# A gather ring of four pairs of rows, with the fifth pair's place left to the first query chunk

## The chip, the cores and the metric

The kernel runs on one core of one Trainium2 chip. The metric is the device time of one execution in microseconds (us), lower is better. Beside the plain runs there is one profiled execution, whose trace gives a start and a duration for every instruction.

## What is computed

Two layers of a hybrid encoder on 256 tokens of 1024 features, in float32, and a final RMS norm. Each layer first adds a mixture of differential attention and a two-directional state-space block to x. Then comes the part on which the change bears, a layer of 128 x 128 = 16384 small experts:

```python
def peer_ffn(h, wq, keys, u_tab, v_tab):
    qry = (h @ wq).reshape(b, s, PEER_HEADS, 2, PEER_HALF)
    sc = jnp.einsum('bshcd,hckd->bshck', qry, keys)
    ...                                    # top 16 of each half, top 16 of their 256 sums: idx, gate
    u = jnp.take(u_tab, ix, axis=0)        # per token 8 heads x 16 = 128 rows
    act = jax.nn.gelu(jnp.einsum('btkd,btd->btk', u, hx), approximate=False)
    wgt = act * gx
    return jnp.einsum('btk,btkd->btd', wgt, jnp.take(v_tab, ix, axis=0))
```

So each of the 256 tokens needs 128 rows of u and 128 rows of v of its own, per layer. They can't be shared, and they all come from HBM.

## The kernel before, in words

Tokens lie on the 128 partitions, in two blocks b = 0 and 1. The tables u and v are put side by side in HBM (peer_uv, 2048 floats a row), so one indirect DMA of GpSimd (POOL) fetches for all 128 tokens of a block the 8 KB row of one of their 128 slots: 1 MiB. Two slots make a **pair**; a block has 64 pairs, a layer 128 (LAYER_PAIRS). The fetched rows go into `ring`, which holds RING_PAIRS = 5 pairs; pair m takes the place m % 5.

Each pair goes through a chain of engines, in the order of m on each:

- POOL issues its two gathers (line 1489), after the index list of the heads is there (experts_ready) and after pair m-5 has been used (pair_used).
- VectorE takes the dot product of each row's u half with h2, one instruction a row (`dots`, line 1379), after both gathers have landed (gathered[q]).
- ScalarE (ACT) applies gelu, the gate, and makes a diagonal matrix from the weights (`weigh`, lines 921, 927, 934).
- TensorE (PE) multiplies the diagonals with the v halves, eight matmuls that add into PSUM (line 693), and reports pair_used.

While pairs flow, VectorE chooses the experts of the heads to come (`route`), in steps between the dots. TensorE computes the queries and key scores that it needs: those of block 0 and the first chunk of block 1 before the first pair (`query_tiles`, line 634, and `key_scores`, line 645), the others (LATE) in pieces behind certain pairs. The order on TensorE at the start of this phase is: query_tiles(0, 1), key_scores(0, 1), the copy of x_tok into PSUM (line 684), then the pairs from 0 on.

The query weights are four chunks of 2 MB. Chunks 1 and 2 pass through the ring of weights w_ring. Chunk 0 (wq0) and chunk 3 (wq3) have places of their own in the arena, a stretch of SBUF that the phases use in turn. wq0 lies 8 x 2 x DM x 4 bytes behind the arena's start, so on the fifth pair's place of the gather ring (16 KB of each partition), and out1 on the fourth pair's. That is why POOL waits before pair 3 for the last product with out1 (mix_full) and before pair 4 for the last use of wq0, the fill of query_tiles(0, 1), which PE reports through bank_full. SP loads wq0 behind the last chunks of the state-space block (line 363) and wq3 at the layer's end (line 370).

Of the kernel before, what the change touches and what calls it, by code (L numbers as in the profile page):

```python
# [20 lines left out]
DEPTH, SEQ, DM = 2, 256, 1024  # L21
P = 128
# [35 lines left out]
FILL = {f: M_NORM2 + i for i, f in enumerate(ROUTE_FILLS)}  # L58
# [23 lines left out]
NCONST = _at  # L82

PAIR = 2
RING_PAIRS = 5
RING = PAIR * RING_PAIRS
BLOCK_PAIRS = SLOTS // PAIR
LAYER_PAIRS = TB * BLOCK_PAIRS
# [36 lines left out]
def encoder_kernel(nc, x, positions, consts, params, w_stream, w_dt, keys_t, norm2_rows, final_row,  # L125
                   peer_uv, out):
    with ExitStack() as ctx:
# [4 lines left out]
        def place(at, name, shape, dt=F32):  # L132

            size = int(np.prod(shape[1:])) * 4
            assert at + size <= end, (name, at + size, end)
            return nc.alloc_sbuf_tensor_at(name, shape, dt, offset=at), (at + size + 31) // 32 * 32
# [41 lines left out]
        arena = base[0]  # L178
        at = arena
        xbc, at = place(at, "xbc", [P, NXBC, SEQ])  # L180
        qk, at = place(at, "qk", [P, 2 * HEADS, SEQ])
        x_fwd, _ = place(at - 2 * HEADS * SEQ * 4, "x_fwd", [P, TB, INNER])
        attT, _ = place(at, "attT", [P, KD, SEQ])
        x_bwd, _ = place(at, "x_bwd", [P, TB, INNER])
        v_tok, at = place(at + KD * SEQ * 4, "v_tok", [P, TB, DM])
        zT, at = place(at, "zT", [P, XT, SEQ])
        partner, _ = place(at - XT * SEQ * 4, "partner", [P, 2 * HEADS, SEQ])
        gateT, at = place(at, "gateT", [P, 2 * KD, SEQ])
        temps = at
        m_mat, at = place(at, "m_mat", [P, 2, 6, HPG, P])  # L190
        cbm, at = place(at, "cbm", [P, 2, 6, P])
        fbuf, at = place(at, "fbuf", [P, 3, HPG, TB, P])
        dt_v, at = place(at, "dt_v", [P, TB, 2 * SH])
        a_v, at = place(at, "a_v", [P, TB, 2 * SH])
        f_col, at = place(at, "f_col", [P, TB, 2 * SH])
        off_b, at = place(at, "off_b", [P, 2 * SH])
# [3 lines left out]
        xn, _ = place(temps, "xn", [P, TB, DM])  # L200
# [5 lines left out]
        r_bc, _ = place(temps + 8192, "r_bc", [P, SEQ])  # L206
        trig, _ = place(temps + 9216, "trig", [P, 4, SEQ])
        pos_i, _ = place(temps + 8192, "pos_i", [P, SEQ], I32)

        o_view = fbuf[:, 0:2].rearrange("p n r b l -> p (n r b l)").rearrange("p (b h e) -> p b h e", b=TB, h=HEADS)  # L210
        cs_rows, _ = place(temps + 20480, "cs_rows", [P, TB, P])


        at = arena
        ring, at = place(at, "ring", [P, RING, 2 * DM])
        out1, _ = place(arena + 6 * 2 * DM * 4, "out1", [P, 4096])
        wq0, _ = place(arena + 8 * 2 * DM * 4, "wq0", [P, 4096])
        wq3, at = place(at, "wq3", [P, 4096])
        h2, at = place(at, "h2", [P, TB, DM])
        sc, at = place(at, "sc", [P, 5, 4, PK])  # L220
        qryT, at = place(at, "qryT", [P, 2, 4, P])
        keys, at = place(at, "keys", [P, 2 * PH, PK])
        g2row, at = place(at, "g2row", [P, DM])
        eq, _ = place(at, "eq", [P, 2, TOPK, TOPK])
        cand, at = place(at, "cand", [P, 2, TOPK, TOPK])
        vals, at = place(at, "vals", [P, 4, TOPK])
        idxs, at = place(at, "idxs", [P, 4, TOPK], U32)
        best, at = place(at, "best", [P, 2, TOPK])
        posn, at = place(at, "posn", [P, 2, TOPK], U32)
        idxf, at = place(at, "idxf", [P, 4, TOPK])  # L230
        ab_u, at = place(at, "ab_u", [P, 2, 2 * TOPK], U32)
        ab_f, at = place(at, "ab_f", [P, 2, 2 * TOPK])
        selv, at = place(at, "selv", [P, 2, 2 * TOPK])
        ex_i, at = place(at, "ex_i", [P, TB, SLOTS], U32)
        gsum, at = place(at, "gsum", [P, TB, PH])
        gate_w, at = place(at, "gate_w", [P, TB, PH, TOPK])
        act_u, at = place(at, "act_u", [P, TB, SLOTS])
        gel, at = place(at, "gel", [P, TB, SLOTS])
        wgt, at = place(at, "wgt", [P, TB, SLOTS])
        diag, at = place(at, "diag", [P, 2 * PAIR, P])  # L240
# [10 lines left out]
        def sem(name, per_layer):  # L251
            return Count(once(name), per_layer)
# [20 lines left out]
        bank_full = sem("bank_full", FILLS)  # L273
# [52 lines left out]
        experts_ready = sem("experts_ready", len(PARTS))  # L326
        gathered = [once(f"gathered{q}") for q in range(RING_PAIRS)]
        dots_done = sem("dots_done", LAYER_PAIRS)
# [48 lines left out]
        def _(pe):  # L377
# [5 lines left out]
            for L in range(DEPTH):  # L383
# [296 lines left out]
                for b in range(TB):  # L680
# [6 lines left out]
                    for k in range(BLOCK_PAIRS):  # L687
                        m = BLOCK_PAIRS * b + k
                        pe.wait_ge(diag_ready.sem, diag_ready.at(L, m + 1))
                        for s in range(PAIR):  # L690
                            slot = PAIR * (m % RING_PAIRS) + s
                            for n in range(2):
# [736 lines left out]
        @block.gpsimd  # L1429
        def _(pool):  # L1430
            def wait(sig, n, L):
                pool.wait_ge(sig.sem, sig.at(L, n))


            for L in range(DEPTH):

                pool.wait_ge(x_ready.sem, x_ready.at(L, 1))
                pool.memset(partner[:], 0.0).then_inc(partner_clear.sem, 1)
                wait(partner_clear, 1, L)
                for i in range(4):  # L1440
                    wait(bank_empty, M_QK + 2 * i + 2, L)
                    for c0 in (0, HD):
                        for to, source in ((c0, c0 + ROPE // 2), (c0 + ROPE // 2, c0)):
                            pool.dma_start(partner[to:to + ROPE // 2, 4 * i:4 * i + 4, :],
                                           qk[source:source + ROPE // 2, 4 * i:4 * i + 4, :])\
                                .then_inc(partner_loaded[i].sem, 16)

                wait(rows_copied, 1, L)
                pool.dma_start(rows_dram[L], cs_rows[0:2 * SH].rearrange("p b l -> p (b l)")).then_inc(rows_stored.sem, 16)  # L1449
                pool.wait_ge(rows_stored.sem, rows_stored.at(L, 16))  # L1450
                wait(bank_full, M_ATT + 4, L)
                def add_squares(g):

                    wait(ysq_ready, g + 1, L)
                    if g > 1:
                        pool.wait_ge(ysq_added.sem, ysq_added.at(L, g - 1))
                    pool.tensor_tensor(xbc[:, 0:2, :], xbc[:, 0:2, :], xbc[:, 2 * g:2 * g + 2, :], ALU.add)\
                        .then_inc(ysq_added.sem, 1)

                for n in range(F_UNITS):  # L1460
                    g, d = divmod(n, 2)
                    if d == 0 and g >= 6:
                        add_squares(g - 5)
                    if n >= 3:
                        gf, df = divmod(n - 3, 2)
                        pool.wait_ge(diff_ready.sem, diff_ready.at(L, 4 * gf + 2 * df + 2))
                        pool.wait_ge(offexp_done.sem, offexp_done.at(L, 2 * gf + df + 1))
                    row = d * SH + HPG * g
                    slot, _ = unit(L, g, d)
                    pool.dma_start(fbuf[:, slot].rearrange("p r b l -> p (r b l)"),  # L1470
                                   rows_dram[L:L + 1, row:row + HPG, :].rearrange("o r t -> o (r t)")
                                   .broadcast_to([P, HPG * TB * P])).then_inc(f_loaded[slot], 16)
                for g in range(3, GROUPS):
                    add_squares(g)

                for p, (b, h0, nh) in enumerate(PARTS):
                    pool.wait_ge(experts_ready.sem, experts_ready.at(L, p + 1))
                    for i in range(nh * TOPK // PAIR):
                        m = BLOCK_PAIRS * b + h0 * TOPK // PAIR + i
                        q = m % RING_PAIRS  # L1480
                        if m == 3:
                            pool.wait_ge(mix_full.sem, mix_full.at(L, 12))
                        if m == 4:
                            pool.wait_ge(bank_full.sem, bank_full.at(L, FILL["q", 0, 1] + 1))
                        if m >= RING_PAIRS:
                            pool.wait_ge(pair_used.sem, pair_used.at(L, m - RING_PAIRS + 1))
                        for s in range(PAIR):
                            j = TOPK * h0 + PAIR * i + s
                            pool.indirect_dma_start(ring[:, PAIR * q + s, :], None, peer_uv,  # L1489
                                                    bass.IndirectOffsetOnAxis(ap=ex_i[:, b, j:j + 1], axis=0))\  # L1490
                                .then_inc(gathered[q], 16)
# [88 lines left out]
```

## Time and profile before

| | us |
|---|---|
| median of 3 runs | 2359.17 (2358.14 to 2359.28) |
| profiled execution | 2360.61 |
| its span, first to last instruction | 2357.8 |
| busy in the span: PE, VectorE, ACT, POOL | 2055.4, 1347.5, 758.7, 565.6 |
| mean granted TensorE clock | 0.987 |

The kernel moves 706.28 MB by DMA, of which the software queue, that is the gathers, takes 554.87 MB. Busy times of engines overlap, so none of them is the time of the kernel; a stretch is bound by the engine or the transfers that the others wait for there. A row of the timeline tells when one instruction began and how long it took, and in brackets how long its engine had been idle and what ended that idle time.

### The profile page before, as it was taken

The page shows a single profiled execution, that of the slowest core. Times are in us where ns is not written, and L with a number is a line of the kernel's source. Part 1 is how long each engine was busy: PE and PEld are TensorE (multiplying, and loading weights), DVE is VectorE, ACT ScalarE, POOL GpSimd, SP SyncE. Part 2 cuts the span into 40 slices and gives each one's busy share as a digit, 9 for nine tenths or more (in the row PEclk, how much of TensorE's full clock was granted, in tenths as well). Part 3 has the DMA queues.
Part 4 walks back from the last instruction along what each step waited for, and adds up shares of the span by engine and source line. Part 5 has one row for each costly group of instructions (what it writes and reads, how often), then busy time and mean ns, then how long its engine had stood idle before and what let it go on. Part 6 is the DMA issues. An engine that isn't in the chain of part 4 may idle for free.

```text
span 2357.8 us, 23073 instructions
## 1 busy us (share of the span) xinstructions
PE 2055.4 (87%) x8224; PEld 1312.6 (56%) x8224; DVE 1347.5 (57%) x3260; ACT 758.7 (32%) x2029; POOL 565.6 (24%) x598
## 2 busy tenths in 40 slices
PE   7999999999888787777789999999998888777775
PEld 6688888864444332222276888888644444322222
DVE  2367268148765576574423762781486765766644
ACT  2143257023333233323221432560233333233232
POOL 1000002014333333333210000020143333343331
PEclk9999999999999999999989999999999999999999
DMA  5423444559999999999723334445699999999996
GB/s 192 147 108 143 171 168 163 205 230 421 421 423 420 421 422 421 421 421 422 329 81 143 122 129 171 170 161 205 258 422 421 421 422 421 422 421 421 422 421 258
DMA packets 91426, 706.28 MB, mean 300 GB/s; under 512 B 10769, under 2 KB 10897, under 8 KB 16817
## 3 DMA queue, kind: packets, MB, share of 16 engines
q0 software_dynamic: 79424, 554.87, 57.1%
q1 hardware_dynamic: 11168, 146.29, 16.2%
q10 hardware_dynamic: 720, 3.67, 0.5%
q8 instruction: 64, 1.05, 0.2%
q14 instruction: 50, 0.40, 0.0%
HBM read 702.56 MB, written 1.18 MB: 298 GB/s over the span
## 4 chain that ended last, share of the span: by engine, by line
PE 53%; DMA 32%; DVE 7%; ACT 3%; issue 2%; POOL 2%; DVEq 0%; POOLq 0%; SPq 0%; ACTq 0%
DMA ring<-in_peer_uv,ex_i 31%; PE bank L424 23%; PE bank L693 10%; PE bank L409 7%; DVE ring L1379 5%; PE bank L634 3%; PE bank L600 2%; PE bank L445 2%; POOL ring L1489 2%; PE bank L581 2%; ACT diag L934 1%; ACT wgt L927 1%; PE bank L493 1%; PE bank L545 1%; PE bank L467 1%
## 5 line engine op out<-in xcount | busy, mean ns | idle before, releaser
L693 PE MATMUL bank<-ring,diag 128*128 128x512 f32 x2048 | 952.2, 609 | 253.2 <-ACT diag L934 252.7
L1379 DVE SCALAR_TENSOR_TENSOR ring<-ring,h 128x1024 f32<-128x1024 f32 x512 | 607.1, 1223 | 460.9 <-DMA ring<-in_peer_uv,ex_i 457.1
L693 PEld LDWEIGHTS bank<-ring,diag 128*128 128x128 f32 x2048 | 373.8, 192 | 795.8 <-ACT diag L934 416.5
L1489 POOL DMA_INDIRECT ring<-in_peer_uv,ex_i x512 | 501.8, 980 | 975.9 <-PE bank L693 680.0
L424 PE MATMUL bank<-hT,w_ring 128*128 128x256 f32 x2560 | 570.2, 383 | 1.9 <-ACT hT L724 1.9
L424 PEld LDWEIGHTS bank<-hT,w_ring 128*128 128x128 f32 x2560 | 485.4, 191 | 74.7 <-issue 7.4
L921 ACT ACTIVATE gel<-act_u 128x2 f32<-128x2 f32 x256 | 52.1, 203 | 862.2 <-DVE ring L1379 861.9
L934 ACT ACTIVATE diag<-cst,wgt 128x128 f32<-128x128 f32 x512 | 177.5, 394 | 8.4
L927 ACT ACTIVATE wgt<-gel,gate_w 128x1 f32<-128x1 f32 x512 | 123.0, 287 | 9.5
L1101 DVE SCALAR_TENSOR_TENSOR c_tmp<-xbc,par_all,c_tmp 128x254 f32<-128x254 f32 (+1 forms) x256 | 112.4, 480 | 4.5
L409 PE MATMUL bank<-zT,w_ring 128*128 128x256 f32 x512 | 111.0, 379 | 0.2
L409 PEld LDWEIGHTS bank<-zT,w_ring 128*128 128x128 f32 x512 | 97.1, 190 | 14.1 <-issue 1.0
L1449 POOL DMA_DIRECT2D cs_rows_dram<-cs_rows x2 | 1.1, 572 | 388.6 <-DVE cs_rows L1146 388.6
L1051 DVE TENSOR_TENSOR rot_tmp<-partner,sin_t 128x512 f32<-128x512 f32 x16 | 11.1, 692 | 108.2 <-DMA partner<-qk 107.0
L634 PEld LDWEIGHTS bank<-hT,w_ring 128*128 128x128 f32 x512 | 61.3, 192 | 12.4 <-issue 12.4
L1470 POOL DMA_DIRECT2D fbuf<-cs_rows_dram x32 | 17.2, 538 | 205.0 <-ACT m_mat L839 155.6
L634 PEld LDWEIGHTS bank<-hT,wq 128*128 128x128 f32 x512 | 60.1, 192 | 10.1 <-issue 10.1
L713 ACT ACTIVATE xn<-x_tok 128x1024 f32<-128x1024 f32 x10 | 10.5, 1051 | 165.5 <-DVE x_tok L1256 151.2
L634 PE MATMUL bank<-hT,wq 128*128 128x128 f32 x512 | 61.0, 275 | 0.6 <-issue 0.6
L634 PE MATMUL bank<-hT,w_ring 128*128 128x128 f32 x512 | 61.4, 275 | 0.0
L1099 DVE TENSOR_SCALAR c_tmp<-xbc,par_all 128x256 f32<-128x256 f32 x64 | 23.4, 408 | 65.2 <-ACT xbc L773 65.2
L409 PE MATMUL bank<-attT,w_ring 128*128 128x256 f32 x256 | 55.8, 380 | 2.4 <-ACT attT L811 2.4
(196 smaller groups left out, 1703.8 us busy)
## 6 DMA issues: line engine op xcount, KB each, us to landing
w_ring<-in_w_stream SPq DMA_DIRECT2D x62, 2048.0 KB
fbuf<-cs_rows_dram POOLq DMA_DIRECT2D x32, 512.0 KB, 5.0
wq<-in_w_stream SPq DMA_DIRECT2D x4, 2048.0 KB, 10.1
ring<-in_peer_uv,ex_i POOLq DMA_INDIRECT x512
out<-in_w_stream SPq DMA_DIRECT2D x2, 2048.0 KB, 12.8
keys<-in_keys_t ACTq DMA_DIRECT2D x2, 1024.0 KB, 4.9
x_tok<-in_x SPq DMA_DIRECT2D x1, 1024.0 KB, 4.9
partner<-qk POOLq DMA_DIRECT2D x32, 32.0 KB, 7.0
```

The source lines that it names most:

```text
L409: ins = pe.matmul(two(b0 + j // 2)[:, j % 2, :], w[:, k, j * P:(j + 1) * P], rhs(k), start=(k == 0), stop=(k == ks - 1))
L424: ins = pe.matmul(two(m % 2)[:, j % 2, :], w[:, k, j * P:(j + 1) * P], hT[:, k, :], start=(k == 0), stop=(k == KD - 1))
L445: ins = pe.matmul(bank[m % 2][:], hT[:, k, b * P:(b + 1) * P], w[:, k, :], start=(k == 0), stop=(k == KD - 1))
L581: ins = pe.matmul(two(5 + p)[u * SP_:(u + 1) * SP_, j, l * P:(l + 1) * P], xs[:, s, h * SP_:(h + 1) * SP_], m_mat[:, p, t, r, :], start=(n ...
L634: ins = pe.matmul(to[:, j * P:(j + 1) * P], w[:, k, col:col + P], hT[:, k, b * P:(b + 1) * P], start=(k == 0), stop=(k == KD - 1))
L693: ins = pe.matmul(bank[b0 + n][:], diag[:, PAIR * (m % 2) + s, :], ring[:, slot, DM + n * 512:DM + (n + 1) * 512], start=False, stop=True, ...
L921: act.activation(gel[:, b, j:j + PAIR], act_u[:, b, j:j + PAIR], ACT.Gelu).then_inc(gelu_done.sem, 1)
L927: ins = act.activation(wgt[:, b, j + s:j + s + 1], gel[:, b, j + s:j + s + 1], ACT.Copy, scale=gates[:, j + s:j + s + 1])
L934: ins = act.activation(diag[:, PAIR * (m % 2) + s, :], ident, ACT.Copy, scale=wgt[:, b, j + s:j + s + 1])
L1101: ins = dve.scalar_tensor_tensor(out=dst, in0=src, scalar=w, in1=dst, op0=ALU.mult, op1=ALU.add)
L1379: ins = dve.scalar_tensor_tensor(out=row, in0=row, scalar=1.0, in1=h2[:, b, :], op0=ALU.mult, op1=ALU.mult, accum_out=act_u[:, b, PAIR * k ...
L1489: pool.indirect_dma_start(ring[:, PAIR * q + s, :], None, peer_uv, bass.IndirectOffsetOnAxis(ap=ex_i[:, b, j:j + 1], axis=0))\
```

## The change

The ring holds four pairs in place of five. wq0 no longer lies at a fixed distance on the ring but gets a place behind it, the 16 KB that the fifth pair had, and wq3 and all that follows stay where they were. POOL's wait before pair 4 for the first query chunk of block 1 is taken out. As all places and counts are computed from RING_PAIRS, pair m now takes place m % 4, in VectorE's and TensorE's code too, there are four gathered semaphores, and from m = 4 on POOL waits for the use of pair m-4.

```diff
 PAIR = 2
-RING_PAIRS = 5
+RING_PAIRS = 4
 RING = PAIR * RING_PAIRS
...
         ring, at = place(at, "ring", [P, RING, 2 * DM])
         out1, _ = place(arena + 6 * 2 * DM * 4, "out1", [P, 4096])
-        wq0, _ = place(arena + 8 * 2 * DM * 4, "wq0", [P, 4096])
+        wq0, at = place(at, "wq0", [P, 4096])
         wq3, at = place(at, "wq3", [P, 4096])
...
                         if m == 3:
                             pool.wait_ge(mix_full.sem, mix_full.at(L, 12))
-                        if m == 4:
-                            pool.wait_ge(bank_full.sem, bank_full.at(L, FILL["q", 0, 1] + 1))
                         if m >= RING_PAIRS:
                             pool.wait_ge(pair_used.sem, pair_used.at(L, m - RING_PAIRS + 1))
```

## Rows read from the trace of the kernel before

**Rows 1.** The page: forty slices, DMA busy tenths, its rate, chain by line.
```profile
DMA  5423444559999999999723334445699999999996
GB/s 192 147 108 143 171 168 163 205 230 421 421 423 420 421 422 421 421 421 422 329 81 143 122 129 171 170 161 205 258 422 421 421 422 421 422 421 421 422 421 258
...
DMA ring<-in_peer_uv,ex_i 31%; PE bank L424 23%; PE bank L693 10%; PE bank L409 7%; DVE ring L1379 5%; PE bank L634 3%; PE bank L600 2%; PE bank L445 2%; POOL ring L1489 2%; PE bank L581 2%; ACT diag L934 1%; ACT wgt L927 1%; PE bank L493 1%; PE bank L545 1%; PE bank L467 1%
```

**Rows 2.** Busy time by stretch: length, engines, PEclk, DMA share, GB/s.
```profile
545.40:600.00 54.60, 48.73 (x164) 24.80 (x163) 47.02 (x145) 21.70 (x63) 24.26 (x24) 1.00 1.01 421
1150.00:1172.00 22.00, 15.70 (x35) 6.24 (x35) 9.52 (x16) 6.76 (x25) 3.76 (x4) 1.00 0.74 308
1721.00:1900.00 179.00, 156.03 (x521) 79.24 (x519) 129.85 (x339) 60.78 (x195) 72.66 (x74) 1.00 1.01 421
```

**Rows 3.** Timeline, start of layer 0's pairs: start, us, engine, line, count, idle before.
```profile
522.58 7.38 PE L634 MATMUL bank<-hT,wq 128*128 128x128 f32 x64 [0.29 <-issue]
...
526.16 1.22 DVE L1379 SCALAR_TENSOR_TENSOR ring<-ring,h 128x1024 f32<-128x1024 f32 x1 [3.10 <-DMA ring<-in_peer_uv,ex_i]
...
530.23 0.94 POOL L1489 DMA_INDIRECT ring<-in_peer_uv,ex_i  x1 [8.34 <-PE bank L634]
...
533.42 3.60 PE L693 MATMUL bank<-ring,diag 128*128 128x512 f32 x8
...
537.29 1.36 POOL L1489 DMA_INDIRECT ring<-in_peer_uv,ex_i  x1 [4.74 <-PE bank L693]
...
540.43 1.23 DVE L1379 SCALAR_TENSOR_TENSOR ring<-ring,h 128x1024 f32<-128x1024 f32 x1 [1.32 <-DMA ring<-in_peer_uv,ex_i]
...
542.51 1.10 POOL L1489 DMA_INDIRECT ring<-in_peer_uv,ex_i  x1 [2.62 <-PE bank L693]
...
545.41 1.23 DVE L1379 SCALAR_TENSOR_TENSOR ring<-ring,h 128x1024 f32<-128x1024 f32 x1 [2.24 <-DMA ring<-in_peer_uv,ex_i]
```

**Rows 4.** Timeline, the same place in layer 1.
```profile
1712.88 1.28 POOL L1489 DMA_INDIRECT ring<-in_peer_uv,ex_i  x1 [4.82 <-PE bank L693]
...
1715.96 1.22 DVE L1379 SCALAR_TENSOR_TENSOR ring<-ring,h 128x1024 f32<-128x1024 f32 x1 [1.35 <-DMA ring<-in_peer_uv,ex_i]
...
1718.10 1.04 POOL L1489 DMA_INDIRECT ring<-in_peer_uv,ex_i  x1 [2.69 <-PE bank L693]
...
1720.93 1.22 DVE L1379 SCALAR_TENSOR_TENSOR ring<-ring,h 128x1024 f32<-128x1024 f32 x1 [2.24 <-DMA ring<-in_peer_uv,ex_i]
...
1731.34 1.22 DVE L1379 SCALAR_TENSOR_TENSOR ring<-ring,h 128x1024 f32<-128x1024 f32 x1
```

**Rows 5.** Waits of POOL: us in total, times, longest.
```profile
POOL ring L1489 <- PE bank L634: 17.4, 2, 9.1
```

**Rows 6.** DMA issues: engine, count, KB each, us from issue to landing.
```profile
keys<-in_keys_t ACTq DMA_DIRECT2D x2, 1024.0 KB, 4.9
...
out<-h SPq DMA_DIRECT2D x1, 1024.0 KB, 4.0
```

**Rows 7.** Chain of waits, a lap of one slot: start, us, what.
```profile
731.21 2.39 DVE ring L1379 x4
...
735.12 3.71 PE bank L693 x8
...
739.09 0.94 POOL ring L1489
...
756.08 2.39 DVE ring L1379 x4
```

**Rows 8.** Timeline, a pair that is freed late.
```profile
715.35 1.22 DVE L1379 SCALAR_TENSOR_TENSOR ring<-ring,h 128x1024 f32<-128x1024 f32 x1 [1.26 <-DMA ring<-in_peer_uv,ex_i]
...
725.41 1.90 POOL L1489 DMA_INDIRECT ring<-in_peer_uv,ex_i  x1 [3.03 <-PE bank L693]
```

**Rows 9.** Timeline, last landings of layer 0.
```profile
1162.37 1.23 DVE L1379 SCALAR_TENSOR_TENSOR ring<-ring,h 128x1024 f32<-128x1024 f32 x1 [2.59 <-DMA ring<-in_peer_uv,ex_i]
...
1172.21 1.23 DVE L1379 SCALAR_TENSOR_TENSOR ring<-ring,h 128x1024 f32<-128x1024 f32 x1 [2.54 <-DMA ring<-in_peer_uv,ex_i]
```

## Prediction

> **What bounds the kernel now.** I read the page first, the chain by line and the forty slices. The chain that ended last spends 31% of the span in the gather's transfers, more than in any line of TensorE, and in two stretches of the forty slices the DMA digit is 9 at 421 to 423 GB/s [rows 1]. Cut by stretches, both gather phases look alike: DMA share 1.01 at 421 GB/s, while PE is busy 48.7 of 54.6 us in layer 0 and 156 of 179 us in layer 1 [rows 2]. So in these phases, which run to 1172 us and almost to the end of the span, the transfers set the pace. The DVE rows show that pace: the first dot product of each pair of rows begins when the pair has landed: after 526.16 for the first, 540.43 and 545.41 for the fourth and fifth, 4.98 us apart, each after idle time that a DMA ended [rows 3]. A pair is two gathers of 1 MiB; 2.1 MB at 421 GB/s is 4.98 us. Whatever the ring does, it costs time only if the DMA engines run out of work.
>
> **What the change does to the waits.** Addresses stay: ten rows of 8 KB put wq3 at 80 KB behind the arena's start; eight rows and the 16 KB of wq0 put it there too, and wq0 stays at 64 KB. SP's loads, their waits and all counts of TensorE, ACT and VectorE work are as before. Two things change on POOL. First, pair 4 no longer waits for TensorE's first query chunk of block 1 (done with its matmuls at 529.96, fetch at 530.23). Secondly every pair from 4 on waits for the pair four before it, not five. For pair 4 this is a new wait, on pair 0's accumulation, and TensorE has in its order: that same query chunk, its scores, the copy of x_tok, then pair 0. The accumulation of pair 0 ends at 533.42+3.60 = 537.02, and POOL, released by it, issued pair 5 at 537.29 [rows 3]. So the wait removed was implied by the one that replaces it, and **pair 4 is fetched at 537.29 and not at 530.23, 7.06 us later**. In layer 1 the fetch of pair 5 stands at 1712.88 [rows 4], and pair 4 goes there. In general the fetch of pair m now happens when that of pair m+1 happened before, as long as no landing moves. Queued behind the waiting POOL instruction are only later gathers; whoever waits for them is VectorE's dots. Two waits of 17.4 us in total go [rows 5] and nothing is gained by it, as POOL's time is hidden.
>
> **Does the later fetch starve the DMA engines?** They stay busy if the new fetch reaches them before the pair ahead has been moved. Written with what rows show: (landing of pair m-1) minus (issue of pair m) must be at least the fixed part of a lone transfer, its time beyond bytes over rate.
>
> The fixed part: the lone load of the keys, 1 MiB, takes 4.9 us from issue to landing, and the final store of the same size 4.0 us [rows 6]. 1.05 MB at 421 GB/s is 2.49 us, so the fixed part is **1.5 to 2.4 us**. These are transfers from ACT's and SP's queues; no row shows an indirect gather that finds the engines idle, since weights are on the way even when the first one starts. I take 2.4, the upper of the near ends. The far end: the shortest issue of a gather to its dots that the rows have is 1718.10 to 1731.34, 13.2 us, less 4.97 for its bytes: 8.3 us [rows 4]. It had pairs queued ahead of it, which explains it without any fixed part, so I keep it only as a bound.
>
> The Trainium skill (DMA: Bandwidth & Descriptors, section on the anatomy of one DMA on the gpsimd path) prices just this kind: about 2.0 us plus bytes over 436 GB/s. An estimate from it would put the fixed part at 2.0 in place of 2.4, and would leave every sign below the same; no run here shows it alone.
>
> Steady state, from one lap of a slot [rows 7]. Dots of a pair begin at 731.21, its matmuls end at 735.12+3.71 = 738.83 (7.62 later), POOL issues 0.26 later at 739.09, and dots on the new pair begin at 756.08. That is 24.87 us, five times 4.97; of the 16.99 us from issue to dots, a lone fetch would need 4.97+2.4 = 7.4, and 9.6 is waiting in the queue. With four pairs the lap is 4 x 4.97 = 19.9, the issue still 7.88 after the landing, and 12.0 us are left for a fetch that needs 7.4: **4.6 us of slack** per lap. In the terms of the rule: the pair ahead lands 3 x 4.97 = 14.9 after, 14.9 - 7.9 = 7.0 us of room against 2.4.
>
> Late pairs. Some pairs are freed later, because ACT loads tables for the gates' exponent or a w_ring chunk has pushed the landings: the worst that I find away from the start begins dots at 715.35, and its slot's next issue is at 725.41, 10.06 us later [rows 8]. Room: 14.9 - 10.06 = 4.8 us against 2.4. Still covered.
>
> The start of each layer is the tightest, since pair 0 must wait for TensorE's routing work: 10.9 us from dots to free. Pair 4: landing of pair 3 at 540.43 minus issue 537.29 = 3.14 us; pair 5: 545.41 - 542.51 = 2.90 [rows 3]. Layer 1: 1715.96 - 1712.88 = 3.08 and 1720.93 - 1718.10 = **2.83 us** [rows 4]. Against 2.4 the least margin is 0.4. If the fixed part f were larger, the loss would be f - 2.83 once per layer, not per pair, because a late pair gives the next one more room: f = 4 costs 1.1 + 1.2 = 2.3 us in all, f = 5 costs 4.3.
>
> Sum against the profiled execution (2360.6 us, span 2357.8): steady state 0, late pairs 0, starts 0 (0 to +4.3), the two removed waits 0. That execution lies 1.4 above the median of the runs, 2359.17. I add 0.2 for a margin as thin as 0.4 in four places and forecast **2359.4 us**. If the cover is gone: each us by which a lap exceeds 19.9 costs a quarter us per pair.
>
> **Rivals.** (A) The forecast: deep enough, no measurable change. For it: room of 7.0 against 2.4. (B) Slower, at the start: the later fetch of pair 4 is exposed in full, because the engines take up an emptied software queue as slowly as a queued one. The place is the first lap, the price 7.06 us, taken for layer 1 too, 14.1 in all: 2373.3 us. It decides where the fixed part exceeds some 2.8 us by much; against it is 4.9 us for a whole lone load. (C) Slower, everywhere: what I took for queueing is the time that a gather needs anyway, with that 13.2 us as the fetch. The lap is then 7.62 + 0.26 + 13.2 = 21.1 in place of 19.9, 0.31 per pair, for 250 pairs 78 us: 2437 us. It decides from a fetch of 12.0 us. Against it: two pairs' landings are 4.97 apart while each took 17 us, so fetches overlap; for it, nothing here shows a gather on a drained queue. (D) Faster: near a layer's end the DMA share falls to 0.74 while landings go on, so some of the sixteen engines are done before others; the last two landings take 9.84 us, from 1162.37 to 1172.21, so 4.92 and not 4.97 each [rows 2, 9]. A shorter ring keeps the quick engines from running ahead. If their idling speeds the slow one all along, it is 0.05 x 250 = 12.5 us: 2346.7. Against it: they can idle only by as much as the slow one lags, a small share of the time. That the change doesn't do what it says is, for the removed wait, part of A: it is gone, and a later one stands in its place.
>
> **How the numbers follow.** A 0.84, B (in whole or in part) 0.07, C 0.05, D 0.04. A measurement of this kernel tells some 0.2%, 4.7 us, from no change. A stays within it, D is faster, B and C slower: faster 0.04, same 0.84, slower 0.12. A gives 2359.2 to 2363.5 by the bounds of f; with 1 to 2 us for the spread of the runs (2358.14 to 2359.28, the profiled one 2360.6) and a part of B, the range is 2357 to 2365.5.
>
> **What the profile after would show.** Right: POOL's ninth gather of each layer begins near 537.3 and 1712.9, released by the matmuls on the ring and no more by line 634; dots of the first pairs begin at the same times as before; issue to dots in a lap falls from 17.0 to about 12.0 us; the DMA share in the phases stays 1.01 at 421 GB/s; POOL's idle time for the matmuls grows by about the first lap only. Wrong: DVE rows with more than 4.97 us between first dots at the fifth and sixth pair (B), a DMA share of 0.94 throughout (C), or landings at 4.92 (D). The forecast would also fail if the last landing of a layer moved with the first dots unchanged, as a fast engine held back by the ring was then needed.

## The result, and the profile after

| | kernel before | changed kernel |
|---|---|---|
| median of 20 runs, us | 2358.48 | 2363.34 |
| lowest to highest, us | 2356.14 to 2360.2 | 2357.26 to 2367.59 |
| profiled execution, us | 2360.61 | 2365.32 |

The ratio is 1.0019, with a 95% interval of 1.0012 to 1.0026: the change costs 4.9 us, inside the forecast range, within 0.2% as forecast, but clear of zero. It also makes the time less steady: the runs spread over 10 us in place of 4.

The page of the changed kernel, the same two lines as [rows 1]:

```profile
DMA  5423444569999999999823334445699999999996
...
GB/s 192 147 108 143 170 170 161 205 243 389 421 422 409 417 422 421 418 422 420 359 81 143 124 126 170 170 161 205 265 394 421 421 420 420 421 413 421 414 421 286
```

The rate is lower than before in single slices of the gather phases: 389 in the tenth slice (421 before), 409 in the thirteenth (420), 394 in the thirtieth (422). The loss has a place. The start of layer 0's pairs, as in [rows 3] (POOL's gathers are now line 1487):

```profile
536.33 1.59 POOL L1487 DMA_INDIRECT ring<-in_peer_uv,ex_i  x1 [14.98 <-PE bank L693]
...
538.23 0.94 POOL L1487 DMA_INDIRECT ring<-in_peer_uv,ex_i  x1 [0.30 <-issue]
...
539.66 1.23 DVE L1379 SCALAR_TENSOR_TENSOR ring<-ring,h 128x1024 f32<-128x1024 f32 x1 [1.29 <-DMA ring<-in_peer_uv,ex_i]
...
547.93 1.22 DVE L1379 SCALAR_TENSOR_TENSOR ring<-ring,h 128x1024 f32<-128x1024 f32 x1 [5.53 <-DMA ring<-in_peer_uv,ex_i]
```

POOL begins pair 4's first gather at 536.33, released by the ring's matmuls after 14.98 us of waiting; the wait for line 634 is gone. Dots of pair 3 begin at 539.66, those of pair 4 at 547.93: **8.27 us apart and not 4.97**, with VectorE idle for 5.53 us before them. From issue to dots the fetch took 11.60 us. In layer 1, as in [rows 4], two fetches come late, those of pairs 4 and 5:

```profile
1715.36 1.95 POOL L1487 DMA_INDIRECT ring<-in_peer_uv,ex_i  x1 [15.82 <-PE bank L693]
...
1719.06 1.22 DVE L1379 SCALAR_TENSOR_TENSOR ring<-ring,h 128x1024 f32<-128x1024 f32 x1 [1.29 <-DMA ring<-in_peer_uv,ex_i]
...
1720.58 1.65 POOL L1487 DMA_INDIRECT ring<-in_peer_uv,ex_i  x1 [2.02 <-PE bank L693]
...
1725.34 1.23 DVE L1379 SCALAR_TENSOR_TENSOR ring<-ring,h 128x1024 f32<-128x1024 f32 x1 [3.55 <-DMA ring<-in_peer_uv,ex_i]
...
1732.22 1.22 DVE L1379 SCALAR_TENSOR_TENSOR ring<-ring,h 128x1024 f32<-128x1024 f32 x1 [1.37 <-DMA ring<-in_peer_uv,ex_i]
```

The gaps are 6.28 and 6.88 us, where [rows 4] has 4.97 and 5.43 (pair 5 always begins 0.46 late, for VectorE's own work). The DMA share shows the hole, from 536 to 541 us and in layer 1 from 1712 to 1733. Beside them stand a stretch in the middle and the last 22 us of layer 0's phase, up to its last landing, which is now at 1175.5:

```profile
536.00:541.00 5.00, 5.00 (x25) 3.20 (x24) 3.64 (x8) 1.38 (x5) 2.53 (x2) 1.00 0.77 277
1712.00:1733.00 21.00, 20.71 (x74) 11.04 (x73) 13.24 (x40) 5.11 (x19) 9.25 (x8) 1.00 0.89 344
1733.00:1900.00 167.00, 141.78 (x464) 70.88 (x462) 121.46 (x311) 57.62 (x184) 64.38 (x67) 1.00 1.01 422
1153.30:1175.30 22.00, 15.66 (x35) 6.24 (x35) 9.52 (x16) 6.71 (x25) 5.63 (x6) 1.00 0.90 374
```

0.77 and 0.89, at 277 and 344 GB/s. In the middle it is again 1.01 at 422. In the last 22 us it is 0.90, where [rows 2] has 0.74.

The lap of one slot in the steady state, as in [rows 7]:

```profile
899.47 3.71 PE bank L693 x8
...
903.44 0.94 POOL ring L1487
...
915.43 2.39 DVE ring L1379 x4
...
935.31 2.39 DVE ring L1379 x4
```

Issue to dots 903.44 to 915.43, 11.99 us, and the next lap's dots at 935.31, 19.88 later: four times 4.97.

Adding up the profiled executions by first dots: layer 0's phase from pair 0 to pair 127 takes 650.29 us against 646.05, layer 1's 638.68 against 636.50. Layer 0 loses 3.3 at pair 4 and 1.0 at pair 8, layer 1 loses 1.3, 1.45 and 1.1 at pairs 4, 5 and 8 to 9. Of this 1.7 comes back later, where pauses of about 1 us between landings that the kernel before shows now and then fall away or are shorter. The two phases are 4.24 and 2.18 us longer, 6.4 together; the changed kernel came to its first dots 0.9 us sooner, before anything that the change touches, and the spans differ by 5.4.

### The profile page after: what moved, and what is told of

The parts are those of the page before. It is cut to its first block, busy times and chain, and to the rows that moved or that the text cites. A ratio compares the mean times of both kernels' runs of the same rounds, so it can differ in the third digit from the quotient of the medians.

```text
span 2363.2 us, 23073 instructions
## 1 busy us (share of the span) xinstructions
PE 2053.8 (87%) x8224; PEld 1310.6 (55%) x8224; DVE 1348.1 (57%) x3260; ACT 758.2 (32%) x2029; POOL 564.1 (24%) x598
## 3 DMA queue, kind: packets, MB, share of 16 engines
q8 instruction: 64, 1.05, 0.2%
## 4 chain that ended last, share of the span: by engine, by line
PE 52%; DMA 30%; DVE 9%; ACT 4%; issue 3%; POOL 3%; DVEq 0%; POOLq 0%; SPq 0%; ACTq 0%
DMA ring<-in_peer_uv,ex_i 29%; PE bank L424 23%; PE bank L693 11%; PE bank L409 7%; DVE ring L1379 6%; POOL ring L1487 3%; PE bank L445 2%; ACT diag L934 2%; PE bank L581 2%; PE bank L600 2%; ACT wgt L927 1%; PE bank L634 1%; PE bank L493 1%; PE bank L545 1%; ACT gel L921 1%
## 5 line engine op out<-in xcount | busy, mean ns | idle before, releaser
L1051 DVE TENSOR_TENSOR rot_tmp<-partner,sin_t 128x512 f32<-128x512 f32 x16 | 11.1, 692 | 109.9 <-DMA partner<-qk 108.6
L713 ACT ACTIVATE xn<-x_tok 128x1024 f32<-128x1024 f32 x10 | 10.5, 1051 | 165.5 <-DVE x_tok L1256 151.2
## 6 DMA issues: line engine op xcount, KB each, us to landing
wq<-in_w_stream SPq DMA_DIRECT2D x4, 2048.0 KB, 10.7
```

## The experiments

Two theories. **S**: the loss sits at the layers' starts; pair 4's later fetch meets engines that run dry, and a gather is then slower than the prediction took it. **L**: the loss is spread over the laps of a ring that is too short. (Ratios are to the kernel before, run beside each, with 95% intervals.)

### The start alone, with a ring of five: e1_late4

```diff
 # on the kernel before
                         if m == 4:
-                            pool.wait_ge(bank_full.sem, bank_full.at(L, FILL["q", 0, 1] + 1))
+                            pool.wait_ge(pair_used.sem, pair_used.at(L, 1))
```

> The kernel before, ring of five, with one wait exchanged: pair 4 waits for the use of pair 0 and no more for the query chunk. Only the start differs from before. Theory S (the loss lies at the layers' starts, where pair 4 is fetched 7 us later onto engines that run dry, and a fetch there takes 11.6 us from issue to landing and not the 7.4 of the prediction): dots of pair 4 begin 3 us late in layer 0 and 1 to 3 us late in layer 1, as in the changed kernel; the total is 3 to 6 us over before, ratio 1.0012 to 1.0025. Theory L (the loss is spread over the laps of a ring that is too short): dots of pair 4 are late by under 0.5 us, ratio 1.0000 to 1.0005.

Measured: 2361.61 us in 11 runs, ratio 1.0013 (1.0004 to 1.0022). The start of layer 0, POOL's issue of pair 4 and first dots of pairs 3, 4 and 5:

```profile
537.49 0.94 POOL L1489 DMA_INDIRECT ring<-in_peer_uv,ex_i  x1 [16.14 <-PE bank L693]
...
540.10 1.23 DVE L1379 SCALAR_TENSOR_TENSOR ring<-ring,h 128x1024 f32<-128x1024 f32 x1 [1.24 <-DMA ring<-in_peer_uv,ex_i]
...
546.55 1.22 DVE L1379 SCALAR_TENSOR_TENSOR ring<-ring,h 128x1024 f32<-128x1024 f32 x1 [3.63 <-DMA ring<-in_peer_uv,ex_i]
...
551.98 1.21 DVE L1379 SCALAR_TENSOR_TENSOR ring<-ring,h 128x1024 f32<-128x1024 f32 x1
```

6.45 us from pair 3 to pair 4 in this layer, 7.26 in layer 1, then 5.43 as before. The gaps are 1.5 and 2.3 us over 4.97. So the exchange of the wait alone, which the prediction priced at nothing, costs 3 us of the 5. (Some of layer 1's gap is this profile's own: the granted TensorE clock averaged 0.86 from 1696 to 1708 us there, the 64 matmuls of the query chunk took 9.01 us and not 7.38, and pair 0 was free 12.82 us after its dots and not 11.47. The room was only 1.69 us.) Here pair 5 is issued at once behind pair 4, as its place is free already, and its landing doesn't slip: with the depth of five only one fetch of each layer is late.

### Depth four without the late start: e2_deep_start

```diff
 # on the kernel before
                         if m >= RING_PAIRS:
-                            pool.wait_ge(pair_used.sem, pair_used.at(L, m - RING_PAIRS + 1))
+                            pool.wait_ge(pair_used.sem, pair_used.at(L, m - (4 if m >= 16 else RING_PAIRS) + 1))
```

> The kernel before with its ring of five, its wait of pair 4 and its start, but from pair 16 on POOL waits for the use of pair m-4 instead of m-5, so the depth is four in steady state only. Theory S: no loss, since the room of 7.0 us between issue and the landing ahead stays above the 6.6 that the fixed part of a fetch took at the worst place; ratio 0.9998 to 1.0005, landings 4.97 us apart, issue to dots 12.0 in place of 17.0. Theory L: the whole loss, ratio 1.0012 to 1.0026, with single landings 5.5 us apart.

Measured: 2358.33 us in 11 runs, ratio 0.9999 (0.9990 to 1.0009). Timeline of two first dots in the middle of layer 0, and of the issue that belongs to the second:

```profile
903.60 0.94 POOL L1489 DMA_INDIRECT ring<-in_peer_uv,ex_i  x1 [3.46 <-PE bank L693]
...
910.60 1.23 DVE L1379 SCALAR_TENSOR_TENSOR ring<-ring,h 128x1024 f32<-128x1024 f32 x1 [2.58 <-DMA ring<-in_peer_uv,ex_i]
...
915.54 1.23 DVE L1379 SCALAR_TENSOR_TENSOR ring<-ring,h 128x1024 f32<-128x1024 f32 x1 [2.56 <-DMA ring<-in_peer_uv,ex_i]
```

The dots are 4.94 us apart and the fetch takes 11.94. L falls: a steady depth of four costs nothing that 11 runs can tell. Single laps can still slip (in the profiled execution, which was a long one at 2364.5 us, the gaps at pairs 30 and 48 were 1.5 us over those of before), so four is not a comfortable depth.

### Four tiles moved on TensorE: e5_early_free

```diff
 # on the changed kernel, TensorE
                 wait(bank_empty, FILL["t", 1, 1] + 1, L)
-                query_tiles(0, 1, range(4))
-                key_scores(0, 1)
...
                         ins.then_inc(pair_used.sem, 1)
+                        if m < 4:
+                            query_tiles(0, 1, range(m, m + 1))
+                        if m == 5:
+                            key_scores(0, 1)
                         for t0, qb, first in LATE:
-                            if m in range(first, first + 8, 2):
-                                j = (m - first) // 2
+                            if m in (range(4, 8) if first == 0 else range(first, first + 8, 2)):
+                                j = m - 4 if first == 0 else (m - first) // 2
 # ScalarE copies the chunk after pair 4 and its scores after pair 6, not both after pair 0
```

> The changed kernel, ring of four, with TensorE's order altered at each layer's start: the first query chunk of block 1 is no longer multiplied before pair 0 but one tile behind each of pairs 0 to 3, its scores behind pair 5, and the tiles of the next chunk behind pairs 4 to 7. Only the chunk's own place makes this possible. Pair 0 is then free about 3 us sooner, some 7.5 us after its landing in place of 11, so pair 4's gather has 6 us of room. Theory S: the bubble at pair 4 goes, dots of pair 4 begin 4.97 us after those of pair 3, and the total returns to within 1 us of before, ratio 0.9997 to 1.0005. Theory L: no better than the changed kernel, 1.0012 or more.

Measured: 2365.49 us in 6 runs, ratio 1.0032 (1.0020 to 1.0045), so no better than the changed kernel: what theory L expected, and not S. The total agrees with L, but the places do not. Below are rows of layer 0, pair 4 issued, dots of pairs 3 and 4; then layer 1, pair 9 issued, dots of pairs 8 and 9:

```profile
533.47 0.94 POOL L1490 DMA_INDIRECT ring<-in_peer_uv,ex_i  x1 [12.93 <-PE bank L691]
...
540.01 1.23 DVE L1382 SCALAR_TENSOR_TENSOR ring<-ring,h 128x1024 f32<-128x1024 f32 x1 [1.34 <-DMA ring<-in_peer_uv,ex_i]
...
544.96 1.23 DVE L1382 SCALAR_TENSOR_TENSOR ring<-ring,h 128x1024 f32<-128x1024 f32 x1 [2.21 <-issue]
```

```profile
1735.72 1.89 POOL L1490 DMA_INDIRECT ring<-in_peer_uv,ex_i  x1 [2.14 <-PE bank L691]
...
1740.21 1.22 DVE L1382 SCALAR_TENSOR_TENSOR ring<-ring,h 128x1024 f32<-128x1024 f32 x1 [0.18 <-DMA ring<-in_peer_uv,ex_i]
...
1747.00 1.22 DVE L1382 SCALAR_TENSOR_TENSOR ring<-ring,h 128x1024 f32<-128x1024 f32 x1 [2.85 <-DMA ring<-in_peer_uv,ex_i]
```

At pair 4 of layer 0 the gap is 4.95: that bubble is gone, as S says. But eight pairs in a row now carry a tile each on TensorE, and with it a pair takes 5.22 us from one start of its matmuls to the next where a transfer takes 4.97, so the pairs are freed later and later: in layer 0 pair 0 is free 7.7 us after its dots and pair 6 10.0. In layer 1 something else came on top. With its tiles moved away, TensorE was idle for 3.78 us before pair 0, and the clock granted from 1702 to 1708 us was 0.50, the lower of its two levels (TensorE's row; then the stretch, with PEclk third from the end):

```profile
1702.81 6.54 PE L691 MATMUL bank<-ring,diag 128*128 128x512 f32 x8 [3.78 <-ACT diag L936]
...
1702.00:1708.00 6.00, 5.19 (x6) 2.19 (x7) 3.77 (x9) 2.10 (x8) 0.00 (x0) 0.50 1.02 429
```

Pair 0's eight matmuls took 6.54 us where they take 3.60 to 3.70 elsewhere, and pair 0 was free 10.51 us after its dots and not the expected 7.5. TensorE, with its eight loaded pairs, did not catch up: pair 4 had 3.99 us of room and a gap of 5.36, and pairs 9 to 11 met the same late issue, with 4.5 us of room and 6.8 us from dots to dots at pair 9. The edit moved the bubble and made it larger; so this run doesn't speak for a loss spread over the laps. How much of it is the clock's and how much the tiles' was not separated.

### One tile moved: e6_one_tile, beside e8_after_again

```diff
 # on the changed kernel, TensorE
-                query_tiles(0, 1, range(4))
-                key_scores(0, 1)
+                query_tiles(0, 1, range(3))
...
                         ins.then_inc(pair_used.sem, 1)
+                        if m == 0:
+                            query_tiles(0, 1, range(3, 4))
+                        if m == 2:
+                            key_scores(0, 1)
                         for t0, qb, first in LATE:
-                            if m in range(first, first + 8, 2):
-                                j = (m - first) // 2
+                            begin = first + (1 if first == 0 else 0)
+                            if m in range(begin, begin + 8, 2):
+                                j = (m - begin) // 2
 # ScalarE copies the chunk after pair 1 and its scores after pair 3, not both after pair 0
```

> The changed kernel, ring of four, with a smaller shift in TensorE's order than the run of four tiles: of the first query chunk of block 1 only the fourth tile (2 us) goes behind pair 0 and its scores (1.1 us) behind pair 2; the next chunk's tiles come behind pairs 1, 3, 5, 7 in place of 0, 2, 4, 6. Pair 0 should be free 7.6 us after its landing and not 10.8, and no pair up to 9 later than in the changed kernel, which was what the run of four tiles suffered from. Theory S (the loss is at the starts): landings of pairs 4 and 5 stay within 0.5 us of 4.97 apart, the time is 2 to 5 us under the changed kernel of this job, ratio to before 0.9998 to 1.0008. Theory L (the loss is spread over the laps of a ring of four): no gain over the changed kernel.

> The changed kernel itself, once more beside the others of this job, as the yardstick for the run with one tile shifted. Both theories: ratio 1.0012 to 1.0026. Theory S: landings of pair 4, and of 5 or 8, over 5.5 us after the one before, with a sum of 3 to 5 us a layer over a cadence of 4.97, and single ones afterwards no larger in sum than in the kernel before.

Measured side by side, 11 runs each: one tile moved 2358.36 us, ratio 0.9999 (0.9990 to 1.0008); the changed kernel again 2363.55 us, 1.0020 (1.0011 to 1.0029). In the latter's profile the gaps at pairs 4 and 5 were 6.15 and 6.78 in layer 0, 5.71 and 5.89 in layer 1; over a cadence of 4.97 that is 3.0 and 1.7 us, so in layer 1 less than the 3 to 5 that was expected (the profiled execution was one of the shorter ones, 2361.1 us). With one tile moved (pair 4's issue, dots of pairs 3, 4 and 5; DMA share of the same stretch as above):

```profile
532.43 0.94 POOL L1492 DMA_INDIRECT ring<-in_peer_uv,ex_i  x1 [11.77 <-PE bank L692]
...
538.99 1.22 DVE L1384 SCALAR_TENSOR_TENSOR ring<-ring,h 128x1024 f32<-128x1024 f32 x1 [1.35 <-DMA ring<-in_peer_uv,ex_i]
...
543.95 1.23 DVE L1384 SCALAR_TENSOR_TENSOR ring<-ring,h 128x1024 f32<-128x1024 f32 x1 [2.23 <-DMA ring<-in_peer_uv,ex_i]
...
549.38 1.21 DVE L1384 SCALAR_TENSOR_TENSOR ring<-ring,h 128x1024 f32<-128x1024 f32 x1
```

```profile
536.00:541.00 5.00, 5.00 (x25) 3.24 (x24) 3.58 (x8) 1.38 (x5) 1.88 (x2) 1.00 1.01 416
```

The gaps are 4.96 and 5.43 us (in layer 1 the same), and the share is 1.01 where the changed kernel had 0.77. The fetch took 11.52 us, but it had been issued 6.56 us before pair 3's dots, and 11.52 - 6.56 is 4.96: no gap. This removes the whole loss, with a ring of four throughout. With e1, where the late start alone costs 3 us, and e2, where the depth alone costs nothing, it shows that **the loss is the late issue at the layers' starts and nothing else that these runs can tell**.

### What a drained fetch costs: e3_ring3, e4_alone, e7_direct3

```diff
 # e3: on the changed kernel, every place but the ring's own depth unchanged
-RING_PAIRS = 4
+RING_PAIRS = 3
...
-        ring, at = place(at, "ring", [P, RING, 2 * DM])
+        ring, at = place(at, "ring", [P, 8, 2 * DM])
 # e4: on the changed kernel, POOL
+                        if m == 0:
+                            pool.wait_ge(wq3_loaded.sem, wq3_loaded.at(L, 16))
 # e7: on e3
-                            pool.indirect_dma_start(ring[:, PAIR * q + s, :], None, peer_uv,
-                                                    bass.IndirectOffsetOnAxis(ap=ex_i[:, b, j:j + 1], axis=0))\
+                            row = EXPERTS * L + P * (PAIR * (m % 60) + s)
+                            pool.dma_start(ring[:, PAIR * q + s, :], peer_uv[row:row + P, :])\
```

> The changed kernel with a ring of three pairs (the fourth's place stays empty). Now every fetch finds engines that have run dry, so that lap times give a fetch's own time X from first issue to dots: a lap is 7.9 + X, a pair takes (7.9 + X)/3. If X is 7.4, as the prediction had it: 5.1 us a pair and 30 to 40 us more in all, about 2395. If X is 11.6, as at pair 4 of the changed kernel: 6.5 us a pair, 250 x 1.53 = 380 us more, about 2740 us. Landings evenly apart would say that X is the time of any drained fetch, uneven ones that pair 4 was a special case.

> The changed kernel, but POOL starts each layer's gathers only when the last query chunk (wq3) has landed, so that the first pair meets engines with nothing to do. Question: the fetch of one pair with nothing before it and pairs 1 to 3 close behind it. By the prediction's fixed part of 2.4 us it takes 7.4 us from issue to dots; by the run with a ring of three 10.5 us (most between 9.0 and 12.0). The total should rise by some 12 us a layer, the time by which the first gather is held back (511 to 523 us), less what the weights then take from no gather: 10 to 25 us in all.

> The run with a ring of three, with every gather replaced by a plain load of the same size from the same table, 128 rows of 8 KB that follow one another, issued by POOL on the same queue; so the experts' rows are not those that the reference picks. It tells whether the 10.5 us of a drained fetch come from scattered rows and indices or from the queue. If from the scatter: issue to dots falls to about 7.4 us and the time to 2390 or less. If from the queue and from what starting all engines at once costs: it stays at 9 to 11 us and the time at 2640 to 2710.

Measured, with two runs of each: e3 2709.18 us (1.1486, 1.1465 to 1.1507), e4 2374.55 us (1.0068, 1.0049 to 1.0086), e7 2563.79 us (1.0870, 1.0828 to 1.0912). Pair 3 in e3 is the first whose fetch finds nothing ahead of it (issue, dots):

```profile
535.08 1.02 POOL L1487 DMA_INDIRECT ring<-in_peer_uv,ex_i  x1 [18.64 <-PE bank L693]
...
544.09 1.22 DVE L1379 SCALAR_TENSOR_TENSOR ring<-ring,h 128x1024 f32<-128x1024 f32 x1 [7.54 <-DMA ring<-in_peer_uv,ex_i]
```

9.01 us. The pairs after it are uneven; first dots in the middle of layer 0:

```profile
881.52 1.23 DVE L1379 SCALAR_TENSOR_TENSOR ring<-ring,h 128x1024 f32<-128x1024 f32 x1 [3.21 <-DMA ring<-in_peer_uv,ex_i]
...
888.25 1.23 DVE L1379 SCALAR_TENSOR_TENSOR ring<-ring,h 128x1024 f32<-128x1024 f32 x1 [4.35 <-DMA ring<-in_peer_uv,ex_i]
...
906.07 1.23 DVE L1379 SCALAR_TENSOR_TENSOR ring<-ring,h 128x1024 f32<-128x1024 f32 x1 [4.06 <-DMA ring<-in_peer_uv,ex_i]
...
913.59 1.23 DVE L1379 SCALAR_TENSOR_TENSOR ring<-ring,h 128x1024 f32<-128x1024 f32 x1 [3.18 <-DMA ring<-in_peer_uv,ex_i]
...
923.66 1.27 DVE L1379 SCALAR_TENSOR_TENSOR ring<-ring,h 128x1024 f32<-128x1024 f32 x1 [0.78 <-DMA ring<-in_peer_uv,ex_i]
...
932.58 1.23 DVE L1379 SCALAR_TENSOR_TENSOR ring<-ring,h 128x1024 f32<-128x1024 f32 x1 [4.90 <-DMA ring<-in_peer_uv,ex_i]
```

From 881.52 to 888.25 it is 6.7 us, from 906.07 to 913.59 7.5, from 923.66 to 932.58 8.9. The mean from the times: 350.7 us over 250 pairs is 1.40 a pair, 6.37 us in all, a lap 19.1; the work from dots to the end of the matmuls takes 8.5 us here on average (7.6 to 10.6) and POOL's start 0.3, which leaves about **10.3 us** for a fetch on average. But this is no average of drained fetches: against what was expected, most fetches of e3 were issued before the pair ahead had landed, and part of their time is waiting behind it. In the profile 35 of 250 were issued after it; they took 9.4 us on average (8.7 to 10.7), and all together 10.5. The first pair of e4, whose gathers begin after the weights have landed (POOL's wait and VectorE's):

```profile
518.59 1.01 POOL L1489 DMA_INDIRECT ring<-in_peer_uv,ex_i  x1 [107.44 <-DMA wq<-in_w_stream]
...
528.22 1.23 DVE L1379 SCALAR_TENSOR_TENSOR ring<-ring,h 128x1024 f32<-128x1024 f32 x1 [7.95 <-DMA ring<-in_peer_uv,ex_i]
```

9.63 us. And pair 3 of e7, the same place as in e3, with plain loads of consecutive rows:

```profile
535.40 1.05 POOL L1488 DMA_DIRECT2D ring<-in_peer_uv  x2 [24.04 <-PE bank L693]
...
542.85 1.23 DVE L1379 SCALAR_TENSOR_TENSOR ring<-ring,h 128x1024 f32<-128x1024 f32 x1 [5.74 <-DMA ring<-in_peer_uv]
```

7.45 us. That is what the prediction had for a lone fetch, 7.4. So its two rows [rows 6] were right for what they show, plain transfers, and a gather of the same bytes on the same queue takes 1.6 us longer at this place. On average over the profile e7's fetches take 8.9 us, where e3's take 10.5; its time fell between the two that were expected (2390 or less, 2640 to 2710), as the first fetch fits the one theory and the average lies nearer the other.

The packets in the two traces tell where the 1.6 us lie. POOL spends 1.05 us on both plain loads of a pair and 2.26 on the two gathers (0.94 to 1.02 each and 0.30 between), and the first packet of rows starts 1.25 us after the issue of the plain loads began and 1.72 after that of the gathers: 0.5 us. The rest lies at the end. Sixteen packets of 4 bytes stand behind each transfer, as if one from each DMA engine; behind the second plain load they come within 0.2 us of one another, behind the second gather within 1.3 us (542.42 to 543.75). So the engines finish a gather unevenly, and VectorE waits for the last. Whether that comes from the rows being scattered wasn't separated. e4's total, 16 us over before, holds some bubbles besides the later start: in layer 0 pairs 3 to 5 slipped by 1.3, 1.4 and 1.1 us, while the granted TensorE clock was 0.86 and 0.68 in the stretches from 526 to 532 and to 540 us.

## Why the prediction was right, and where it was not

**The size and the sign of the bounds.** 2363.34 lies in the range of 2357 to 2365.5 and the difference within 0.2%, but 4.9 us is more than the likeliest case allowed for the median, 0.2. What was measured is the upper end of case A, what f = 5 gives (4.3 us). It came from the mechanism that the prediction described, and priced at zero. Of its signs of being wrong the first came true, more than 4.97 us before the fifth pair's dots; the same sign at the sixth tells nothing, as it is 5.43 in the kernel before. That the range held is in part luck: by the prediction's own formula the fixed part of 6.6 us, seen at pair 4, would cost 7.5 us and lead to 2366.7, past the range.

**The replaced wait: right.** Pair 4 was fetched at 536.33, 11.1 us after the first dots at 525.24; in the kernel before pair 5 was fetched 11.1 us after them (537.29 - 526.16). The removed wait was implied by the new one, and nothing was gained from it. e1 shows this by itself.

**The steady lap: right.** 11.99 us from issue to dots, forecast 12.0; lap 19.88, forecast 19.9; DMA share 1.01. But its slack was not 4.6 us. A fetch on idle engines of 9.4 us (e3's average) leaves 2.6, and the long one (11.6 at pair 4) 0.4. That this was enough is e2's and e6's finding, not the prediction's. The late pairs, priced at zero with 4.8 us of room, had 4.0, 4.7 and 4.75 at pairs 40, 41 and 52 of layer 0; the second lost 0.5 us against before, the others nothing.

**The fixed part of a lone fetch: the term that failed.** The prediction took 2.4 us from plain transfers, had 8.3 as the far end, and chose the near one. A gather took 9.63 us alone (fixed part 4.7), 11.60 at pair 4 of the changed kernel (6.6), 9.97 and 11.64 at pairs 4 and 5 of layer 1 (5.0, 6.7), a mean of 10.3 (5.3) in e3. Each of these fixed parts is a time from issue to dots less 4.97. The one of e3 is too high for a drained fetch, as said there; the 35 that count give 4.4. The others at pairs 4 and 5 are read from late landings, so that at a late pair the bubble is the fixed part minus the room by their very making (pair 4 in layer 0: room 539.66 - 536.33 = 3.33, fixed part 6.63, lost 3.30). What tests the rule is the other side: with 6.56 us of room (e6) and 6.54 (e5) at pair 4 there was no gap, with 3.3 and 3.7 there was one. In between, the room alone doesn't decide. Pair 5 of layer 1 had 4.76 us of room in the changed kernel's profile (1725.34 - 1720.58, shown with the result) and lost 1.45 us; pair 52 of layer 0 had 4.75 in the same profile and lost nothing (issue, dots of pairs 51 and 52):

```profile
790.16 1.84 POOL L1487 DMA_INDIRECT ring<-in_peer_uv,ex_i  x1 [10.20 <-PE bank L693]
...
794.91 1.22 DVE L1379 SCALAR_TENSOR_TENSOR ring<-ring,h 128x1024 f32<-128x1024 f32 x1 [1.74 <-DMA ring<-in_peer_uv,ex_i]
...
799.88 1.23 DVE L1379 SCALAR_TENSOR_TENSOR ring<-ring,h 128x1024 f32<-128x1024 f32 x1 [1.26 <-DMA ring<-in_peer_uv,ex_i]
```

So the fixed part is no constant. POOL's part doesn't tell the two cases apart, as its two gathers took 2.90 us at pair 5 and 3.10 at pair 52. Why the fixed part is 4.0 to 4.7 us in some places and 6.6 in others stays open. The rooms of 3.14 and 3.08 us that the prediction read for pair 4 were about right (3.33 and 3.69 measured), and rooms of 2.8 to 3.1 compared with 4.7 or more would have given 1.9 a layer at least. The Trainium skill (DMA: Bandwidth & Descriptors, anatomy of one DMA on the gpsimd path) gives 2.0 us of fixed cost. The plain loads on POOL's queue come near it when nothing is ahead of them (7.45 - 4.97 = 2.5); the gathers don't, at 4.0 to 6.7 in the places shown, and for them the measurement decides.

**Once per layer: partly wrong.** I held that a late pair gives the next one more room, so that f - 2.83 would be paid once. It does give room (4.62 at pair 5 in the second profile of the changed kernel), but the fetch of that pair took 11.4, so it slipped as well. So did one more near pair 8. With five (e1) only the fetch of pair 4 was late.

**The rivals.** B (exposed start, 7.06 a layer) was the right place at a third of its price. C has its point at a fetch of 12.0 us; 9.4, and at worst 11.6, is nearer to it than I gave it credit for, and e3 shows what lies beyond: 350 us for one pair less. D is refuted: the quick engines are held back (share 0.90 in the last 22 us in place of 0.74), and the last landings are 4.98 and 4.93 apart. The larger spread of the changed kernel's runs fits a time that depends on how long a few late fetches take, but no run singles that out.

**No version beats the kernel before.** With one tile moved, the ring of four reaches its time, 0.9999, and wq0 has its 16 KB to itself at no cost. The gather phases are bound by bytes in both.

## What to carry to other kernels

A ring's depth is to be judged by room: the time from the issue of a fetch to the landing ahead of it, against the fixed part of a fetch on drained engines. Take that fixed part from the same kind of transfer; here a gather's was 4.0 to 4.7 us on idle engines where a plain load's was 2.5. And leave a margin: over 6 us of room left no gap at pair 4, under 4 left one of up to 3.3, and in between it went either way. Look at the first lap on its own, where the consumer is late for other reasons: the ring of four was deep enough for nearly all pairs of a layer and too short for a few of the first ten. And look at the clock where an edit takes work away from TensorE: in e5 half of it was granted at such a place.

## What the runs showed of the hardware that was not expected

- A pair of 1 MiB gathers on idle engines took 9.01 and 9.63 us from issue to dots, in the ring of three 9.4 on average where the pair ahead had landed; two plain loads of the same size on the same queue 7.45. In a full queue a pair of gathers costs 4.97.
- POOL spends 0.94 to 2.00 us on a gather's issue and 0.52 on a plain load's.
- Landings go by the slowest of the sixteen DMA engines. Behind pair 3 of the changed kernel twelve of the sixteen had nothing left by 537.7 us, by the packets of the trace, and the last finished at 539.2; dots began at 539.66. Before, the DMA share was 0.74 in the last 22 us of a layer while landings stayed 4.92 to 4.97 apart; with four pairs it was 0.90 there, at the same pace. The deeper ring only let the quick engines run ahead.
